# Local attention: the turn of the probabilities as a product with the identity scaled by the reciprocal row sums

## What is computed

```python
logits = jnp.einsum("bnqhgd,bnkhd->bnhgqk", qb, k_band) * (HEAD_DIM ** -0.5)
logits = jnp.where(mask[None, :, None, None], logits + bias, NEG_INF_2)
sink = sinks.astype(f32).reshape(N_KV_HEADS, Q_PER_KV)[None, None, :, :, None, None]
m = jnp.maximum(jnp.max(logits, axis=-1, keepdims=True), sink)
p = jnp.exp(logits - m)
probs = p / (jnp.sum(p, axis=-1, keepdims=True) + jnp.exp(sink - m))
out = jnp.einsum("bnhgqk,bnkhd->bnqhgd", probs, v_band)
```

## Time and profile before

| | before |
|---|---|
| executions, us | 1246.44, 1248.59, 1248.81 |
| profiled execution, us | 1247.35 |
| its span, us | 1245.5 |
| instructions | 14735 |
| VectorE busy | 62% |
| ScalarE busy | 39% |
| GpSimd busy | 5% |
| DMA, mean GB/s | 116 |

### The profile page before, as it was taken

The page is one execution under the profiler, slowest core; times in us unless marked ns, Lnnn a source line. Parts: engine busy times, 40 slices in busy tenths (PEclk is TensorE's granted clock), DMA queues, the critical chain, the costliest instruction groups (busy, mean ns, idle before and its releaser), DMA issues.

```text
span 1245.5 us, 14735 instructions
## 1 busy us (share of the span) xinstructions
PE 1204.1 (97%) x5913; PEld 940.0 (75%) x5913; DVE 772.1 (62%) x1278; ACT 486.2 (39%) x742; POOL 61.8 (5%) x74
## 2 busy tenths in 40 slices
PE   7999999899999999999999999799899999999998
PEld 5786666468778787878887885477688888888887
DVE  5536574757677776775876596746666543455542
ACT  6244545735322212222275234862444321344320
POOL 0000000013100000000022000025000000000000
PEclk9999999999999999999999999899999999999999
DMA  9311011223465577353235530112222223323122
GB/s 344 138 69 68 35 68 34 102 77 116 163 216 190 188 245 251 127 177 116 62 110 163 185 110 1 68 34 81 88 85 88 78 93 114 102 102 102 70 93 91
DMA packets 31883, 144.66 MB, mean 116 GB/s; under 512 B 3303, under 2 KB 9672, under 8 KB 22600
## 3 DMA queue, kind: packets, MB, share of 16 engines
q1 hardware_dynamic: 31816, 143.73, 33.3%
HBM read 136.90 MB, written 6.82 MB: 115 GB/s over the span
## 4 chain that ended last, share of the span: by engine, by line
PE 76%; DVE 3%; ACT 2%; issue 1%; DVEq 0%
PE bank L133 24%; PE bank L134 23%; PE bank L135 23%; PE bank L2538 1%; PE bank L683 1%; PE bank L1864 1%; PE bank L2505 1%; DVE squares L362 0%; PE bank L2547 0%; PE bank L198 0%; DVE keep L1655 0%; PE bank L2581 0%; PE bank L2569 0%; PE bank L1857 0%; ACT prob L2168 0%
## 5 line engine op out<-in xcount | busy, mean ns | idle before, releaser
L133 PE MATMUL bank<-xhi_ffn,w_hi_part 128*128 128x512 f32 x704 | 278.0, 395 | 4.3 <-DVE xlo_ffn L234 4.3
L121 ACT ACTIVATE w_hi_part<-w_raw 128x2048 fp32r<-128x2048 f32 (+1 forms) x95 | 164.0, 1726 | 287.6 <-PE bank L135 285.8
L134 PE MATMUL bank<-xlo_ffn,w_hi_part 128*128 128x512 f32 x704 | 275.9, 392 | 0.0
L135 PE MATMUL bank<-xhi_ffn,w_lo_part 128*128 128x512 f32 x704 | 274.9, 391 | 0.0
L127 DVE TENSOR_TENSOR w_lo_part<-w_raw,w_hi_part 128x2048 fp32r<-128x2048 f32 (+1 forms) x95 | 197.4, 2078 | 83.4 <-ACT w_hi_part L121 80.1
L133 PEld LDWEIGHTS bank<-xhi_ffn,w_hi_part 128*128 128x128 f32 x704 | 132.6, 188 | 35.1 <-issue 6.6
L135 PEld LDWEIGHTS bank<-xhi_ffn,w_lo_part 128*128 128x128 f32 x704 | 132.7, 188 | 30.3
L134 PEld LDWEIGHTS bank<-xlo_ffn,w_hi_part 128*128 128x128 f32 x704 | 132.2, 188 | 28.4 <-issue 0.2
L362 DVE SCALAR_TENSOR_TENSOR squares<-bank,param,squares 128x511 f32<-128x511 f32 x88 | 63.9, 747 | 84.6 <-ACT squares L345 83.1
L133 PE MATMUL bank<-hhi_half,w_hi_part 128*128 128x512 f32 x240 | 94.1, 392 | 0.0
L134 PE MATMUL bank<-hlo_half,w_hi_part 128*128 128x512 f32 x240 | 93.4, 389 | 0.0
(11 more groups left out here) (377 smaller groups left out, 1867.7 us busy)
## 6 DMA issues: line engine op xcount, KB each, us to landing
mod_w<-in_w_mod SPq DMA_DIRECT2D x32, 768.0 KB, 4.3
w_raw<-in_w_gu SPq DMA_DIRECT2D x22, 1024.0 KB, 6.3
w_raw<-in_w_down SPq DMA_DIRECT2D x32, 704.0 KB, 4.1
w_raw<-in_w_up SPq DMA_DIRECT2D x22, 1024.0 KB, 4.8
w_raw<-in_w_in_f SPq DMA_DIRECT2D x8, 1024.0 KB, 5.1
w_raw<-in_w_out SPq DMA_DIRECT2D x8, 1024.0 KB, 4.8
w_raw<-in_w_in SPq DMA_DIRECT2D x5, 1024.0 KB, 4.9
x<-in_x SPq DMA_DIRECT2D x8, 256.0 KB, 6.1
```

What stands on the lines that cost most here:

```text
L121: act.activation(k.whi[:, slot, 0:width], k.raw[:, slot, 0:width], ACT.Copy).then_inc(k.w_hi, 1)
L133: pe.matmul(out, whi, xhi, start=first, stop=False)
L134: pe.matmul(out, whi, xlo, start=False, stop=False)
L135: return pe.matmul(out, wlo, xhi, start=False, stop=last)
```

## The change

The probabilities stay as the exponentials left them. In `normalise` VectorE writes, for each head of the round, the identity with its rows multiplied by the reciprocal row sums into a new tile `inverse` (two pairs of 128x128 in turn). `turn` multiplies each block of the probabilities, as the weights, by this diagonal matrix. The result is the same: the transposed block with each column divided by its sum. `normalise` also waits, from round 2 on, until the turn two rounds before is done.

```diff
@@ names of tiles @@
+        inverse = over("inverse_diagonals", [P, 4, P], xlo_at + 6240 + 8192)
@@ def normalise(p) @@
                 dve.reciprocal(k.rsum[:, 2 * p:2 * p + 2], k.rsum[:, 2 * p:2 * p + 2]).then_inc(l_inverted, 1)
                 dve.wait_ge(l_inverted, p + 1)
+                if p >= 2:
+                    dve.wait_ge(l_turned, p - 1)
                 for r in range(2):
-                    _, _, at, _ = local(p, r)
-                    s, u = 2 * (p % 3) + r, 2 * p + r
-                    dve.tensor_scalar(prob2[:, s, at:256], prob2[:, s, at:256], k.rsum[:, u:u + 1], None,
+                    u = 2 * p + r
+                    dve.tensor_scalar(inverse[:, 2 * (p % 2) + r, :], k.ident, k.rsum[:, u:u + 1], None,
                                       ALU.mult).then_inc(l_normed, 1)
@@ def turn(p) @@
-                        mm = pe.transpose(turn_bank[0 if p >= ONE_TURN else p % 2][:, 256 * r + P * b:256 * r + P * b + P],
-                                          prob2[:, 2 * (p % 3) + r, at + P * b:at + P * b + P], k.ident)
+                        mm = pe.matmul(turn_bank[0 if p >= ONE_TURN else p % 2][:, 256 * r + P * b:256 * r + P * b + P],
+                                       prob2[:, 2 * (p % 3) + r, at + P * b:at + P * b + P],
+                                       inverse[:, 2 * (p % 2) + r, :], start=True, stop=True)
```

## The result

| | before | after |
|---|---|---|
| executions beside each other | 20 | 20 |
| median, us | 1248.28 | 1251.97 |
| lowest to highest, us | 1244.44 to 1250.33 | 1246.70 to 1255.95 |
| profiled execution, us | 1247.35 | 1248.21 |
| its span, us | 1245.5 | 1246.4 |

The ratio is 1.0027, with a 95% interval of 1.0017 to 1.0037: 0.27%, some 3.4 us, slower. The profiled execution of the changed kernel is one of its fast ones, 3.8 us under its own median. It must not be read as typical, and much of this case turns on that.

A forecast was written before the change was run, and what follows sets the result against it. TensorE, busy 97% of the span and carrying 76% of the chain, was taken as the bound. Added turn cost 2.7 us minus 1.7 for the vanished clock fall gave +1.0, so 1249.6 us, range 1246.3 to 1252.5.

The forecast's parts named there:

- Rival 1: Round 2's lag products: the clock falls as before, so the whole 2.7 us is paid, 1251.3 us; 28%.
- the clock falling in part A again: Sign of a wrong forecast: granted clock low again between rounds 1 and 2, where it was forecast at 1.00.
- part A: 759 to 779 us, TensorE's own work: longer turns of rounds 1 to 4 add 1.24 us.
- VectorE, -0.14 us in each of three rounds: Rounds 1, 7 and 10: scalings of 128 instead of 256 columns save 0.14 us each on the chain.
- The added wait costs nothing: In normalise from round 2 on: the wait for the turn two rounds before is always already met, cost nothing.
- A product is two records of 0.112 us: In the turns on TensorE: each product takes 0.223 us, so a turn of four takes 0.89 in a stream.
- The sum of 2.7 us: Local attention, 751 to 822 us: total added with the clock as it was, 1.5 + 1.2 us.
- part C: 802 to 822 us, TensorE's gate products and turns of rounds 12 to 15: longer turns add 1.23 us.
- ScalarE's slack of 1.15 us takes the extras of rounds 5 and 6: 779 to 802 us: extras of 0.29 and 0.45 us delay only a ScalarE copy, with slack before round 9's exponentials.
- Rounds 10 and 11 at the low clock, 1.79 us a turn, and TensorE takes over the chain: After the standstill: turns of four take 1.79 instead of 1.11 us, gate products start at 804.6; shift 1.5 us.
- The early fall is gone, -1.7 us: Clock fall at 764 us, round 2's lag products: disappears as idle time shrinks to 1.17 us, saving 1.70 us.

The follow-up runs named there:

- second profile: Profile of the changed kernel run again with no edit; that run's median 1250.84 us, ratio 1.0021 to the kernel before.
- experiment 3: Changed kernel with the turn put back to a transpose with the plain identity, diagonal made but unread; median 1246.85 us, ratio 0.9986 to the kernel before.
- experiment 9: Kernel before with idle products at four places, diagonals made in place of scaled probabilities, turn still a transpose; mean 1242.3 us, ratio 0.9953.
- experiment 11: Changed kernel with idle products at four places and every product of the turn issued twice; mean 1254.7 us, ratio 1.0052 to the kernel before.
- filled kernels: Kernel before and changed kernel, each with unread idle products at four places; means 1242.3 and 1244.4 us, ratios 0.9955 and 0.9971.
- experiment 6: Kernel before with unread idle products at four places (680 us, before round 1, in the standstill, 875 us); mean 1242.3 us, ratio 0.9955.
- Experiment 12: Kernel before with idle products at four places and three more ahead of round 11's turn; median 1241.32 us, ratio 0.9954.
- experiment 5: Kernel before with seven unread idle products in the standstill ahead of round 10's turn; median 1247.75 us, ratio 0.9993.

## Why the prediction was right and wrong

The measured median, 1251.97 us, lies in the range of 1246.3 to 1252.5, near its top, and 2.4 us above the 1249.6 forecast. By the bound of 0.2% the change is slower, to which I had given 27%, and I had 66% on the same. Rival 1 has the time (1251.3), though not for its reason alone. The range held because it had been drawn to hold rival 1 and 1 us of spread, not because the sum was right: two of its terms erred, both towards too fast. And its own sign of being wrong, the clock falling in part A again, was there in the second profile.

- *VectorE, -0.14 us in each of three rounds:* right in the profiles, -0.39 to -0.41 us in pairs at full clock (65.79 against 66.18 and 66.20, 69.71 against 70.10). The times of experiment 3 would have it larger, those of experiment 9 can't tell.
- *The added wait costs nothing:* right. Experiment 3 is not slower than before, and no profile shows the wait.
- *A product is two records of 0.112 us:* right, by experiment 11 and by the turns of 0.89 us.
- *The sum of 2.7 us:* mis-sized, 3.53 at full clock. The term that failed is the turn that does not follow lag or gate products. I replaced 0.60 and 0.59 (rounds 3 and 13) by the stream's 0.89, and the profile has 1.09 to 1.10; I replaced 0.37 (round 12) by 0.45, and it has 0.64. The pause that the transposes had there stayed. After a wait I had 1.04, and it is 1.13 to 1.15 in round 1 and 1.14 in round 15. So part A is 1.56 instead of 1.24, part C 1.73 instead of 1.23.
- *ScalarE's slack of 1.15 us takes the extras of rounds 5 and 6:* right, but only just. The turn of round 5 takes 1.09 us, like that of round 13, so they are about 0.49 and 0.45 us instead of 0.29 and 0.45, and VectorE comes 0.14 earlier; next to nothing of the slack is left. In the profile after, VectorE's row maxima for round 9 (789.02 + 0.17) are ready as ScalarE comes free:

```profile
789.02 0.17 DVE L2398 TENSOR_SCALAR nmax<-nmax 128x2 f32<-128x2 f32 x1
```

```profile
789.22 0.51 ACT L2169 ACTIVATE prob<-prob,nmax 128x257 f32<-128x257 f32 x1
```

- *Rounds 10 and 11 at the low clock, 1.79 us a turn, and TensorE takes over the chain:* the chain is right in both profiles of the changed kernel. The turn of round 10 took 2.08 us in both. The clock rose sooner than I had it: the turn of round 11 took 1.18 us in one and 1.72 in the other.
- *The early fall is gone, -1.7 us:* this is the step that failed. It took one execution's fall for a property of the kernel. The changed kernel fell there in one of its two profiles, with the same idle time, and over all seven profiles without a filling there the fall came in two of four with products and two of three with transposes. Over all executions the changed kernel's low time is 1.6 +- 1.1 us less than before, which at 0.44 to 0.47 us for one is -0.7 +- 0.5 us, not -1.7. And the price before was one profile's too.

Together: +3.5 - 0.7 = +2.8 us, beside 3.1 +- 0.6 measured as the difference of means. In the filled kernels the difference is 2.0 +- 0.4 us with 2.7 us less low time (1.5 against 4.2), and 3.2 +- 0.3 at equal low time, which agrees with the 3.5 of the profiles.

The Trainium skill, "TensorE: Matmul & The Clock Gate", part 4, has the rule that transposes do not count as busy time for the clock gate the way products do. The mean low times would fit it: the filled kernels with transposes have 4.1 to 5.3 us, those with products 1.5 and 2.1. But the profiles do not place the difference at the turns. Of the four profiles with transposes and all fillings only that of experiment 6 has a low stretch in the local part, and the one at about 220 us, far ahead of the attention, is in kernels of both kinds. Experiment 12 gets to 2.1 +- 1.1 us with transposes. So the rule is not shown here and not refuted. The Trainium skill, same page, Terms, also calls the transpose mode four times faster for 32-bit. The rows on the chain do not show that: 0.44 against 0.89 us, a factor of 2 in a stream.

## What to carry to other kernels

Folding a scaling into a transpose moves work from VectorE to TensorE; where TensorE carries the chain, ask for the price in records: here two for one, which by the profiles cost 3.9 us and saved 0.4. A profile is one execution, and a fall of the clock in it is a draw. Before pricing it, look at the spread of the executions against their mean clock, or fill the idle places with products that nobody reads and compare both kernels so. Here the fillings were worth more (0.45%) than the change under study cost (0.27%).

## What was not expected of the hardware

- Low time goes with most of the spread of this kernel (correlation 0.90, 0.96 in the changed one): 0.44 to 0.47 us of span per us of low time, and 1243 to 1253 us for one and the same program. With four fillings the spread is 1240.6 to 1243.2 us.
- Filling the standstill alone took 8 us off the low time and hardly anything off the run, since much of that low time was idle or hidden behind VectorE, by the timeline of experiment 5. Low time was dear here only where TensorE was on the chain and busy.
- A turn of four behind the 64-row scores or the 32-row products of L683 costs 0.15 to 0.16 us more than behind the lag products as transposes, and 0.20 to 0.21 us more as products, at the same records. Its cause was not looked for.
